# Who builds the gated one-hot rows of the PEER stage: VectorE or GpSimd

## The reference, cut to what matters

```python
top_s, top_i = lax.top_k(s, 16)                      # 16 best keys in each half, per head
cand_i = top_i[..., 0, :, None] * 128 + top_i[..., 1, None, :]
best_s, pos = lax.top_k(cand_s, 16)                  # 16 best pairs
expert = take_along_axis(cand_i, pos)                # expert number = 128 * i + j
gate = softmax(best_s)
act = gelu(einsum('td,thkd->thk', h, u[expert]))
y = einsum('thk,thkd->td', gate * act, v[expert])
x = x + gate2 * y
```

## Time and profile before

| | before |
|---|---|
| median of three runs | 4074.81 us |
| the profiled execution | 4082.18 us |
| its span | 4080.4 us |
| TensorE busy | 3734.0 us (92%) |
| VectorE busy | 2635.2 us (65%) |
| ScalarE busy | 1361.3 us (33%) |
| GpSimd busy | 600.2 us (15%) |
| one-hot rows with gate on VectorE, L1536 | 768 instructions, 215.0 us |

### The profile page before, as it was taken

One profiled execution on the slowest core, in us unless ns is written; L12 is line 12 of the kernel. 1 busy time (PEld: TensorE's weight loads), 2 busy tenths in 40 slices (PEclk: granted clock), 3 DMA queues, 4 the chain that ended last, 5 costly groups with the idle time before them and its releaser, 6 DMA issues. The chain is left out here.

```text
span 4080.4 us, 59457 instructions
## 1 busy us (share of the span) xinstructions
PE 3734.0 (92%) x20964; PEld 3311.5 (81%) x20964; DVE 2635.2 (65%) x5387; ACT 1361.3 (33%) x1743; POOL 600.2 (15%) x516
## 2 busy tenths in 40 slices
PE   5899988788589699799999999999979999999999
PEld 3687876656378599688888888888879999999999
DVE  4133443456543488567777777778768787788887
ACT  2133333355421311124242433333323333333332
POOL 0000000000000000031322232222112222232221
PEclk8999999999789799899999999999989999999999
DMA  7311111111133211475959586867799999999997
GB/s 285 114 51 57 39 53 33 40 47 36 69 132 109 94 36 41 153 235 163 316 170 307 188 283 202 270 222 252 229 339 347 347 346 348 341 371 348 345 347 273
DMA packets 373361, 813.77 MB, mean 199 GB/s; under 512 B 30784, under 2 KB 207808, under 8 KB 369728
## 3 DMA queue, kind: packets, MB, share of 16 engines
q1 hardware_dynamic: 299456, 542.91, 38.3%
q0 software_dynamic: 73728, 268.47, 19.1%
HBM read 681.76 MB, written 129.50 MB: 199 GB/s over the span
## 5 line engine op out<-in xcount | busy, mean ns | idle before, releaser
L80 PE MATMUL s_ps_a<-back_dense_hi,s_u_hi 128*128 128x512 f32 (+1 forms) x2048 | 714.5, 349 | 41.9 <-DVE s_u_lo L1528 27.0
L80 PE MATMUL c_ps_y<-c_wa_hi,c_v_hi 128*128 128x384 f32 x2048 | 687.2, 336 | 30.4 <-DVE c_wa_lo L1860 30.4
L81 PE MATMUL s_ps_a<-back_dense_lo,s_u_hi 128*128 128x512 f32 (+1 forms) x2048 | 697.3, 340 | 0.0
L82 PE MATMUL s_ps_a<-back_dense_hi,s_u_lo 128*128 128x512 f32 (+1 forms) x2048 | 693.9, 339 | 0.0
L82 PE MATMUL c_ps_y<-c_wa_hi,c_v_lo 128*128 128x384 f32 x2048 | 685.8, 335 | 0.0
L81 PE MATMUL c_ps_y<-c_wa_lo,c_v_hi 128*128 128x384 f32 x2048 | 685.7, 335 | 0.0
L1840 ACT ACTIVATE c_v_hi<-c_v_raw 128x1024 fp32r<-128x1024 f32 x256 | 272.2, 1063 | 656.9 <-PE c_ps_y L82 632.8
L1468 POOL DMA_INDIRECT s_row<-in_u_rows,back_expert x128 | 159.5, 1246 | 2158.3 <-DVE back_expert L1630 1716.6
L80 PEld LDWEIGHTS s_ps_a<-back_dense_hi,s_u_hi 128*128 128x128 f32 x2048 | 391.3, 191 | 89.8 <-DVE s_u_lo L1528 27.3
L1858 DVE TENSOR_TENSOR c_v_lo<-c_v_raw,c_v_hi 128x1024 fp32r<-128x1024 f32 x256 | 313.8, 1226 | 196.5 <-ACT c_v_hi L1840 176.5
L82 PEld LDWEIGHTS s_ps_a<-back_dense_hi,s_u_lo 128*128 128x128 f32 x2048 | 388.7, 190 | 46.9
(11 more groups left out here) (317 smaller groups left out, 6763.3 us busy)
## 6 DMA issues: line engine op xcount, KB each, us to landing
c_v_raw<-in_v SPq DMA_DIRECT2D x256, 512.0 KB
s_u_raw<-in_u SPq DMA_DIRECT2D x130, 512.0 KB
act_scratch<-s_a SPq DMA_DIRECT2D x128, 384.0 KB
gm_scratch<-s_gm SPq DMA_DIRECT2D x48, 1024.0 KB
c_a<-act_scratch SPq DMA_DIRECT2D x256, 192.0 KB
c_g<-gm_scratch SPq DMA_DIRECT2D x256, 192.0 KB
a_w<-in_w_ada SPq DMA_DIRECT2D x24, 1024.0 KB, 7.6
q_raw<-in_w_pq SPq DMA_DIRECT2D x17, 512.0 KB, 3.5
```

The costliest lines, as they stand in the source:

```text
L80: nc.tensor.matmul(out, w_hi, x_hi, start=first, stop=False)
L81: nc.tensor.matmul(out, w_hi, x_lo, start=False, stop=False)
L82: return nc.tensor.matmul(out, w_lo, x_hi, start=False, stop=last)
```

## The change

The four `one1` instructions of each group move from VectorE's `hot` into GpSimd's program. Their operands and the buffers stay as they are. A new semaphore `gated` counts the groups that GpSimd has done, and TensorE waits for it beside `hot_done`. GpSimd's program, a plain list of fetches before, is now laid out along the bodies: after 13 fetches at the start it follows VectorE's places of `rows.take`, with one fetch for each row. In a unit with one-hot groups its order is: group 0, group 1, a fetch, group 2, group 3, a fetch. Before the first group of a body it waits for the whole choice, copied `sel_t` included.

```diff
@@ activate_and_select, GpSimd
-            gp.wait_ge(step, STEPS)
-            for n in range(2 * SEL):
+            def gather(n):
                 if n >= R:
                     gp.wait_ge(used, n - R + 1)
                 gp.indirect_dma_start(...).then_inc(row_in[n % R], 16)
+
+            def gated_rows(tt, g):
+                if g == 0:
+                    gp.wait_ge(step, STEPS * (tt + 2))
+                gp.wait_ge(g_ready, GROUPS * tt + (g + 1))
+                for i in range(GT):
+                    t = g * GT + i
+                    last = nc.gpsimd.tensor_scalar(one1[:, g % 2, i], iota[:], sel_t[:, 0, t:t + 1], sel_t[:, 2, t:t + 1], ALU.is_equal, ALU.mult)
+                last.then_inc(gated, 1)
+
+            gp.wait_ge(step, STEPS)
+            for n in range(R + LEAD_UNITS):
+                gather(n)
+            taken = LEAD_UNITS
+            for tt in range(DENSE):
+                for j in range(BODY):
+                    if HOT <= j < HOT_END:
+                        for q in range(QUARTERS):
+                            gated_rows(tt, (j - HOT) * QUARTERS + q)
+                            if q % 2 == 1:
+                                gather(taken + R)
+                                taken += 1
+                    else:
+                        for _ in range(UNITS[j]):
+                            if taken + R < 2 * SEL:
+                                gather(taken + R)
+                            taken += 1
+            for n in range(taken + R, 2 * SEL):
+                gather(n)
@@ activate_and_select, VectorE
             def hot(tt, g):
                 dve.wait_ge(g_ready, GROUPS * tt + (g + 1))
-                nc.vector.tensor_tensor(one2[:, g % 2], ..., ALU.is_equal)
-                for i in range(GT):
-                    t = g * GT + i
-                    last = nc.vector.tensor_scalar(one1[:, g % 2, i], iota[:], sel_t[:, 0, t:t + 1], sel_t[:, 2, t:t + 1], ALU.is_equal, ALU.mult)
-                last.then_inc(hot_done, 1)
+                nc.vector.tensor_tensor(one2[:, g % 2], ..., ALU.is_equal).then_inc(hot_done, 1)
@@ activate_and_select, TensorE
                             pe.wait_ge(hot_done, GROUPS * tt + (g + 1))
+                            pe.wait_ge(gated, GROUPS * tt + (g + 1))
                             pe.wait_ge(g_copied, GROUPS * tt + (g + 1))
```

More of the change, by code:

```diff
@@ L1400, in activate_and_select @@
         used, y_zero, dots_gelu, w_done = (m.sem(x) for x in ("used", "y_zero", "dots_gelu", "w_done"))
+        gated = m.sem("gated")
         u_in, a_stored = ([m.sem(f"{x}{b}") for b in range(2)] for x in ("u_in", "a_stored"))
@@ L1469, in _ @@
                                       in_offset=bass.IndirectOffsetOnAxis(ap=keep.expert[:, 0, n % SEL:n % SEL + 1], axis=0)).then_inc(row_in[n % R], 16)
+            def gated_rows(tt, g):
[23 more added lines that the diff above has]
+                            taken += 1
+            assert taken == 2 * SEL - LEAD_UNITS
+            for n in range(taken + R, 2 * SEL):
+                gather(n)
         @block.scalar
@@ L1532, in hot @@
                 nc.vector.tensor_tensor(one2[:, g % 2], iota[:].rearrange("p (o n) -> p o n", o=1).broadcast_to([P, GT, NK]),
-                                        sel_t[:, 1, g * GT:(g + 1) * GT].rearrange("p (t o) -> p t o", o=1).broadcast_to([P, GT, NK]), ALU.is_equal)
-                for i in range(GT):
-                    t = g * GT + i
-                    last = nc.vector.tensor_scalar(one1[:, g % 2, i], iota[:], sel_t[:, 0, t:t + 1], sel_t[:, 2, t:t + 1], ALU.is_equal, ALU.mult)
-                last.then_inc(hot_done, 1)
+                                        sel_t[:, 1, g * GT:(g + 1) * GT].rearrange("p (t o) -> p t o", o=1).broadcast_to([P, GT, NK]), ALU.is_equal)\
+                    .then_inc(hot_done, 1)
             places = iota[:, 0:TOPK].rearrange("p (o a) -> p o a", o=1).broadcast_to([P, SEL, TOPK])
```

## The result

The changed kernel takes 4384.9 us (median of 4 runs, 4383.7 to 4386.7) where the kernel before took 4077.4 on the same chip: a ratio of 1.0755, interval 1.0738 to 1.0773. That is 307 us slower, outside the stated range (4044 to 4320). It went the way that was forecast, five times as far as the forecast's 60 us.

A forecast was written before the change was run, and what follows sets the result against it. TensorE was taken to bound the stage, waiting 0.8 us a unit for VectorE's late rows. Net +46 us from group 2 and +16 from first units, rounded to +60 on 4082.2, gave 4142 profiled, median 4135; range 4044 to 4320.

The forecast's parts named there:

- What bounds the kernel: TensorE, with one 0.8 us stall before group 1 in 42 units, none in a body's first; removal worth 34 us.
- x: Time of each of the 768 instructions added on GpSimd: taken as 0.43 us, ends 0.10 and 0.94.
- the deciding step: Fetch ahead of group 2 waits for VectorE's row; group 2 late by 1.90 us against 0.80 removed: +46 us.
- the switch at x = 0.55: One-hot units: GpSimd has room up to about this instruction time; from there its throughput binds.
- the rival behind it: GpSimd's throughput binds the one-hot units: about 4280 us at 0.7 us an instruction, 4415 to 4525 at 0.94; chance 0.18.
- The hold: GpSimd's `tensor_scalar`, like its fetches, waits for the end of a two-input VectorE instruction running beside it.
- Twice VectorE's time: Skill's rule for two-input elementwise work on GpSimd: 0.51 us an instruction, result some 13 us above the forecast.
- VectorE held by GpSimd: Delay of VectorE's two-input instructions in one-hot units: taken as 0, at most 0 to 2x in a unit.
- Third wait on TensorE: TensorE's added wait, 192 times: taken as 0 because matmuls are queued ahead; 11 us if all exposed.
- First unit of a body: Group 0 is 2.2 us late, group 2 adds about 0.5: 6 x 2.7 = 16 us over six bodies.

The follow-up runs named there:

- K = 1: Changed kernel, but GpSimd makes one of each group's four gated rows, VectorE three: 4127.4 us with a fetch ahead of group 2, 4075.5 with both fetches last.
- K = 2: Changed kernel, but GpSimd makes two of each group's four gated rows, VectorE two: 4229.7 us with a fetch ahead of group 2, 4134.0 with both fetches last.
- K = 4: Changed kernel, GpSimd making all four gated rows of a group: 4384.9 us with a fetch ahead of group 2, 4425.1 with both fetches last.

## Why the prediction was wrong

- **What bounds the kernel: right.** One stall of 0.8 us in a unit, behind `u_lo`. I priced it at 34 us; taking it away alone gave 42 (36 to 51 by the interval), and by the traces 36 lie in the one-hot units. One reading was too narrow: the first unit of a body has no stall in the body I looked at, but up to 0.9 us in others, 2 us in all.
- **The term that was mis-sized is x.** "I take x = 0.43, nearer to the same operation on VectorE than to the fetch." It is 0.78, nearer to the fetch's 0.94. The choice between VectorE's 0.255 and the fetch's 0.94, nearly four times apart, rested on likeness of the operation, when here the engine was the better guide: its only real work in the trace was at 0.94, and the memset showed only that small things can be quick.
- **With it the deciding step changed.** "This is the step that decides" was the fetch ahead of group 2. The text had the switch at x = 0.55 and the rival behind it: 16x + 2.48 + 2.35 to 4.7. At 0.78 that is 17.3 to 19.7 us; 18.8 was measured, and the sign that the text named for this rival, stalls on every group, is there. So the kernel got slower as forecast, but for the rival's reason and not for mine. I gave that rival 0.18. Its time for x = 0.78 would have been 4290 to 4405 (4.5 to 6.9 us x 48 on 4075), and the range ended at 4320. That end was too low by the text's own formula, which at x = 0.75 gives 4268 to 4381.
- **The fetch step itself is real.** It costs 52 us where GpSimd has the time to be waiting (K = 1), 96 at K = 2, and nothing where it hasn't (K = 4; there the other order was slower still).
- **The hold: right, and at least half of the loss.** A fetch's wait for a two-input instruction carried over to `tensor_scalar`. The rule quoted from the Trainium skill (SBUF — State Buffer, Practical consequences) agrees: 3.07 us for an instruction of 0.78, and 137 us less when those instructions were cut to 8 columns. What I hadn't allowed for is that three in a row hold it through.
- **Twice VectorE's time: too low here.** The Trainium skill (GPSIMD Engine Reference, 4.1 Engine selection) says about twice for two inputs and line rate for one. Here a `tensor_scalar` of 128 columns takes 0.78 against VectorE's 0.255, three times, much of it not going by columns.
- **VectorE held by GpSimd: nothing, right.** It is held a little, a `one2` up to 1.05 us instead of 0.69 and one `u_lo` 1.59 instead of 1.23, but it has 317 us of waiting for TensorE before its `one2` to spare.
- **Third wait on TensorE: nothing, right.** With all three waits, groups that are in time follow at 2.99 to 3.00 us (K = 1, fetches last).
- **First unit of a body:** 2.7 forecast, 8 measured, mostly for the same reason: GpSimd's rows take longer here too, and all four groups are late instead of two.

## What to carry to other kernels

Before work moves to an idle engine, add up that engine's time for one turn of the loop, waits for the shared interface included, and set it against the loop's; "15% busy" says nothing where the work has to be done within 12 us. For GpSimd, price a small instruction from GpSimd's own rows, and count it as held by each two-input instruction of VectorE that runs beside it. And look first whether the late work is late because of its place: moving one line gave 42 us, where moving 768 instructions cost 307.

## What the runs showed of the hardware

**TensorE's clock fell behind some of the stalls.** In the kernel with K = 2 and a fetch between, TensorE idles 2.23 us ahead of group 2 in every unit. Columns of the first view as above, the clock third from the end; then TensorE behind one of these stalls:

```profile
1906.80:1912.30 5.50, 3.26 (x20) 2.82 (x21) 4.74 (x10) 1.10 (x1) 4.08 (x4) 1.00 0.50 163
1912.30:1917.00 4.70, 4.69 (x21) 4.18 (x22) 1.81 (x3) 1.07 (x1) 4.40 (x5) 0.64 0.19 43
```

```profile
1912.31 1.34 PE L1770 MATMUL s_ps_g<-s_one 128*128 128x128 f32 x8 [2.23 <-issue]
1915.37 0.63 PE L80 MATMUL s_ps_a<-back_dense_hi,s_u_hi 128*128 128x512 f32 x1
1915.79 0.63 PE L81 MATMUL s_ps_a<-back_dense_lo,s_u_hi 128*128 128x512 f32 x1
1916.94 1.05 PE L1770 MATMUL s_ps_g<-s_one 128*128 128x128 f32 x8
1918.06 0.39 PE L81 MATMUL s_ps_a<-back_dense_lo,s_u_hi 128*128 128x512 f32 x1
1918.29 0.39 PE L82 MATMUL s_ps_a<-back_dense_hi,s_u_lo 128*128 128x512 f32 x1
```

The 512-column matmuls come at a pitch of 0.42 us (1915.37 to 1915.79) instead of 0.23 (1918.06 to 1918.29), the lower of the clock's two levels (1.2 instead of 2.4 GHz), and the quarter takes 4.63 us instead of 3.0. After the same stall one unit later the clock stayed at 1.00 and the unit was 14.7 us instead of 16.3. So a stall can cost 1.6 us more than its length. In the changed kernel the stage's clock is 0.94 instead of 0.99, but the slow quarters lie in time that GpSimd needs anyway: its own row adds up to the unit without them. What decides whether it falls was not tried.

**A one-input instruction of VectorE doesn't hold GpSimd.** At K = 2 (fetches last) VectorE alternates two-input instructions with `tensor_scalar`, and GpSimd gets in at the latter:

```profile
1907.22 0.68 DVE L1563 TENSOR_TENSOR s_one<-s_iota,s_sel_t 128x512 f32<-128x512 f32 x1
1907.82 0.74 DVE L1567 TENSOR_SCALAR s_one<-s_iota,s_sel_t 128x128 f32<-128x128 f32 x2
1908.39 1.21 DVE L1682 SCALAR_TENSOR_TENSOR s_row<-s_row,s_tok 128x1024 f32<-128x1024 f32 x1
```

```profile
1906.41 2.07 POOL L1477 TENSOR_SCALAR s_one<-s_iota,s_sel_t 128x128 f32<-128x128 f32 x1
1908.47 2.32 POOL L1477 TENSOR_SCALAR s_one<-s_iota,s_sel_t 128x128 f32<-128x128 f32 x1
```

The first ends at 1908.48, so its own 0.78 began at 1907.70, just as `one2` (1907.22 + its pitch of 0.60) gave way to the `tensor_scalar`; the next waits for the row and the `one2` behind it.
